# Half-size products for the first matrix product of the channel mixers' second passes

## The reference, cut to what matters

```
h   = rmsnorm(x, norm_ffn_g[layer]) * (1.0 + sc2) + sh2
hid = jnp.square(jax.nn.relu(jnp.einsum('bsd,df->bsf', h, w_ff1[layer])))   # 1024 -> 4096
x   = x + g2 * jnp.einsum('bsf,fd->bsd', hid, w_ff2[layer])                 # 4096 -> 1024
...
m = jnp.einsum('bd,de->be', jax.nn.silu(c), w) + b     # modulation: sh, sc, g for both halves of a layer
```

## Time and profile before

| | us |
|---|---|
| three timed runs | 2747.79, 2771.42, 2804.4 |
| median | 2771.42 |
| the profiled execution's own time | 2761.02 |
| its span on the slowest core (core 2) | 2759.5 |
| spans of all cores | 2687.8 to 2759.5 |
| PE / DVE / ACT / POOL busy | 2679.8 / 1831.6 / 1351.7 / 865.0 |

### The profile page before, as it was taken

One profiled execution on the slowest core, in us unless ns is written; L12 is line 12 of the kernel. 1 busy time (PEld: TensorE's weight loads), 2 busy tenths in 40 slices (PEclk: granted clock), 3 DMA queues, 4 the chain that ended last, 5 costly groups with the idle time before them and its releaser, 6 DMA issues.

```text
span 2759.5 us, 49737 instructions; the slowest of 8 cores (2687.8 to 2759.5 us)
## 1 busy us (share of the span) xinstructions
PE 2679.8 (97%) x16860; PEld 1576.9 (57%) x16860; DVE 1831.6 (66%) x3259; ACT 1351.7 (49%) x2155; POOL 865.0 (31%) x956
## 2 busy tenths in 40 slices
PE   3999999999999999999999999998999999999998
PEld 1444444445656766676675444444766666676675
DVE  3577776777656667777767666676656666666766
ACT  4787777783445443223225655544445443334323
POOL 4455555442424421000002443413423430112111
PEclk9899999999999999999999988898999999999999
DMA  9743444447453359757536556554254347222321
GB/s 191 152 124 104 108 107 108 108 108 153 105 153 96 93 154 184 173 128 173 124 95 158 153 148 171 139 135 125 77 140 136 93 139 167 83 87 77 131 84 62
DMA packets 126410, 348.12 MB, mean 126 GB/s; under 512 B 13904, under 2 KB 16464, under 8 KB 115280
## 3 DMA queue, kind: packets, MB, share of 16 engines
q1 hardware_dynamic: 107008, 266.29, 31.1%
q0 software_dynamic: 19152, 78.65, 17.6%
HBM read 301.90 MB, written 117.44 MB: 152 GB/s over the span
## 4 chain that ended last, share of the span: by engine, by line
PE 91%; DMA 3%; DVE 2%; issue 2%; ACT 1%; POOL 1%; DVEq 0%; SPq 0%; ACTq 0%; POOLq 0%
PE ps L743 47%; PE ps L1171 28%; PE ps L1011 4%; PE ps L1394 4%; PE ps L1340 4%; PE ps L984 2%; DMA sb_arena<-w_in 1%; DMA xs<-sb_arena 1%; DMA sb_arena<-xs 1%; POOL sb_arena L1387 1%; PE ps L888 0%; PE ps L1377 0%; ACT L412 0%; DVE sb_arena L1364 0%; PE ps L694 0%
## 5 line engine op out<-in xcount | busy, mean ns | idle before, releaser
L743 PE MATMUL ps<-sb_arena 128*128 128x512 bf16 x6144 | 1425.3, 390 | 5.1 <-DMA sb_arena<-w_in 5.1
L743 PEld LDWEIGHTS ps<-sb_arena 128*128 128x128 bf16 x6144 | 608.5, 100 | 733.5 <-issue 179.4
L1171 PE MATMUL ps<-sb_arena 128*128 128x256 bf16 x7168 | 804.6, 274 | 6.5 <-DVE sb_arena L1139 6.5
L1171 PEld LDWEIGHTS ps<-sb_arena 128*128 128x128 bf16 x7168 | 704.7, 98 | 108.9 <-issue 8.8
L692 POOL TENSOR_TENSOR sb_arena<-sb_arena 128x512 f32<-128x512 f32 (+1 forms) x259 | 359.9, 1390 | 968.7 <-ACT sb_arena L689 942.5
L1183 DVE SCALAR_TENSOR_TENSOR sb_arena<-ps,sb_arena 128x256 f32<-128x256 f32 x1280 | 526.7, 477 | 193.2 <-PE ps L1171 188.7
L1133 ACT ACTIVATE sb_arena<-ps 128x512 f32<-128x512 f32 x512 | 304.0, 595 | 681.0 <-PE ps L743 626.3
L1139 DVE TENSOR_TENSOR sb_arena<-sb_arena 128x512 bf16<-128x512 f32 x288 | 225.6, 783 | 336.2 <-ACT sb_arena L1133 335.8
L1152 DVE TENSOR_TENSOR sb_arena<-sb_arena 128x1024 bf16<-128x1024 bf16 x320 | 258.3, 843 | 47.5 <-ACT sb_arena L1136 39.2
L689 ACT ACTIVATE sb_arena<-sb_arena 128x512 f32<-128x512 f32 x273 | 168.0, 622 | 58.6 <-POOL sb_arena L692 32.3
L412 ACT ACT_TABLE_LOAD x124 | 159.1, 1283 | 46.0 <-PE ps L743 33.8
(11 more groups left out here) (129 smaller groups left out, 1906.1 us busy)
## 6 DMA issues: line engine op xcount, KB each, us to landing
xs<-sb_arena SPq DMA_DIRECT2D x320, 256.0 KB, 4.7
sb_arena<-xs SPq DMA_DIRECT2D x160, 512.0 KB, 6.0
sb_arena<-w_ff POOLq DMA_DIRECT2D x32, 1024.0 KB, 12.1
sb_arena<-ada_w POOLq DMA_DIRECT2D x72, 256.0 KB, 5.6
sb_arena<-x SPq DMA_DIRECT2D x64, 256.0 KB, 3.9
hs<-sb_arena SPq DMA_DIRECT2D x16, 1024.0 KB, 12.3
sb_arena<-hs SPq DMA_DIRECT2D x16, 1024.0 KB, 8.8
sb_arena<-xs SPq DMA_DIRECT2D x64, 256.0 KB, 4.1
```

The lines of the kernel that those rows point to most:

```text
L743: parts = [(lambda e, kc=kc: e.matmul(bk(B), w[:, kc, col0:col0 + 128], hT[:, kc, :], start=kc == 0, stop=kc == 7), [wb, hb[kc]], c_mm(512 ...
L1171: parts.append((lambda e, m=m, fc=fc, h=h, r=r: e.matmul(bk(Bm)[:, h * H:(h + 1) * H], w[:, fc, m * 128:(m + 1) * 128], r, start=h == 0 an ...
```

## The change

In the second pass of each layer (p = 1) the first product is made by seven half-size products as well. The K of 1024, the 2048 hidden channels and the 512 positions are each halved. `first_sums` makes the sums of the weight quarters once a pass, 10 instructions of 128x2048 elements, four of them on GpSimd. `prepare` adds 5 sums of h for each tile, in place or into a buffer `Th`. `ff1_halves` replaces `ff1`: for each of 8 pairs of output blocks a bank "grows" through three visits, with reads between them, and what has to be shared between banks is gathered in a small buffer `part`. h now lives in one buffer for all tiles, instead of two in turn.

The second pass's `ff2` is rewritten in the same per-bank form: products 2 and 5 into two halves of a bank (ScalarE copies one, VectorE adds the other), product 1 shared, then 4 with 3 and 7 with 6 onto the same bank. It has the same 224 matmuls; 24 adds into x and 8 helper adds replace the 40 adds. The first pass keeps both of its functions (the old `ff2` is called `ff2_plain`).

Around it: slots are dealt out anew, so the quarters of w_ff2 for a second pass go to slots that the pass before uses to its end, and all w_in loads of `phase_m1` come at the end of the second pass. One of the five sums of w_ff2 for a second pass moves to GpSimd. 32 of the 48 modulation vectors are made in layer 0's first pass (7 a tile), 16 in its second (4 a tile). `finish` takes channels in another order and stores some parts on ScalarE's queue. `TP` becomes 52.5 for the first and 49.0 for the second pass.

```diff
-        TP = 52.5
+        TP = (52.5, 49.0)
 
         FFS = {(0, 0): ((5, 4, 3, 6), (1, 2, 0, 9), (10, 11, 7)),
-               (0, 1): ((12, 13, 14, 15), (5, 4, 3, 6), (1, 2, 0)),
-               (1, 0): ((0, 1, 2, 4), (5, 6, 7, 9), (10, 11, 12)),
-               (1, 1): ((13, 14, 15, 3), (0, 1, 2, 4), (5, 6, 7))}
+               (0, 1): ((12, 13, 14, 15), (10, 11, 7, 9), (1, 2, 0), (5, 4, 3), 6),
+               (1, 0): ((0, 1, 2, 7), (9, 6, 12, 13), (14, 15, 10)),
+               (1, 1): ((3, 4, 5, 11), (14, 15, 10, 13), (9, 6, 12), (0, 1, 2), 7)}
+        FUSED = (0, 3)
+        FADD = 4
+        POOLED1 = ((7, 0), (6, 0), (7, 1), (6, 1))
+        POOLED2 = (7,)
...
+            return out
+
+        def first_sums(l, w1, key):
+
+            homes = FFS[l, 1][3]
+            out = {}
+            for i, home in zip((2, 5, 1), homes):
+                lo = slot_lo[home]
+                v = view(lo, [128, 2, 4, 512], BF16)
+                out[i] = [(v[:, g], G.buf("f%d_%d_%d" % (i, l, g), lo + 4096 * g, lo + 4096 * g + 4096))
+                          for g in range(2)]
+            q = {}
+            for g in range(2):
+                for name, i, h in (("11", g, 0), ("12", g, 1), ("21", 2 + g, 0), ("22", 2 + g, 1)):
+                    q[name, g] = (w1[i][0][:, 4 * h:4 * h + 4, :], w1[i][1][h])
+            for g in range(2):
+                for n, (i, x, y, op) in enumerate(((2, "21", "22", ALU.add), (5, "11", "12", ALU.add),
+                                                   (1, "11", "22", ALU.add), (7, "12", "22", ALU.subtract),
+                                                   (6, "21", "11", ALU.subtract))):
+                    d = out[i][g] if i in (2, 5, 1) else q[x, g]
+                    eng = "pool" if (i, g) in POOLED1 else "dve"
+                    G.add(eng, lambda e, d=d, x=q[x, g], y=q[y, g], op=op: e.tensor_tensor(
+                        out=d[0], in0=x[0], in1=y[0], op=op),
+                          [q[x, g][1], q[y, g][1]], [d[1]], key + 12.0 * g + 0.1 * n, 1.25 if eng == "dve" else 4.7)
+            out[7], out[6] = ([q[k, g] for g in range(2)] for k in ("12", "21"))
+            out[3], out[4] = ([q[k, g] for g in range(2)] for k in ("11", "22"))
             return out
...
+                    Th = o["Th"]
+                    for n, (dst, x, y, op) in enumerate(((Th[1], (0, 0), (1, 1), ALU.add), (Th[6], (0, 0), (0, 1), ALU.add),
+                                                         (Th[7], (1, 0), (1, 1), ALU.add),
+                                                         (None, (0, 1), (1, 1), ALU.subtract),
+                                                         (None, (1, 0), (0, 0), ALU.subtract))):
+                        xa, xbufs = hq(ti, *x)
+                        ya, ybufs = hq(ti, *y)
+                        da, dbufs = (dst[0], [dst[1]]) if dst else (xa, xbufs)
+                        dve(lambda e, xa=xa, ya=ya, da=da, op=op: e.tensor_tensor(out=da, in0=xa, in1=ya, op=op),
+                            xbufs + ybufs, dbufs, key + 30 + 0.1 * n, 0.6)
                     load(ti, key + 15, (2, 3, 0, 1), after)
...
+            def ff1_halves(ti, b):
+                flat = hid.rearrange("p a c t -> p (a c) t")
+                Th, F = o["Th"], w1
+                grow, mid, grow_ops = [None] * 8, [None] * 4, [[], [], [], []]
+
+                def product(B, col, i, m, start=False):
+                    w, wb = F[i][m // 4]
+                    parts = []
+                    if i not in Th:
+                        kh, nh = {2: (0, 0), 5: (1, 1), 3: (0, 1), 4: (1, 0)}[i]
+                        r, rb = hq(ti, kh, nh)
+                    else:
+                        r, rb = Th[i][0], [Th[i][1]] * 4
+                    for kc in range(4):
+                        parts.append((lambda e, kc=kc, r=r, w=w: e.matmul(
+                            bk(B)[:, col:col + H], w[:, kc, (m % 4) * 128:(m % 4) * 128 + 128], r[:, kc, :],
+                            start=start and kc == 0, stop=kc == 3, skip_group_check=True), [wb, rb[kc]], c_mm(H)))
+                    return parts
+
+                def part(m):
+                    v, pb = o["part"][(m // 2) % 3]
+                    return v[:, m % 2, :], pb[m % 2]
+
+                def first(m, k):
+                    B = grow[m] = bank("ff")
+                    op = pe(product(B, 0, 2, m, True) + product(B, H, 5, m), [B], k, barrier[-4:])
+                    grow_ops[m // 2].append(op)
+                    t, tb = part(m)
+                    act(lambda e: e.activation(out=t, in_=bk(B)[:, 0:H], func=AF.Copy), [B], [tb], k - 20, c_act(H, True))
+                    dve(lambda e: e.tensor_tensor(out=t, in0=bk(B)[:, H:TT], in1=t, op=ALU.add), [B, tb], [tb], k - 20,
+                        0.34)
+                    return op
...
+                def second(m, k):
+                    B, q = grow[m], m % 2
+                    pe(product(B, 0, 4, m) + product(B, H, 3, m), [B], k)
+                    act(lambda e: e.activation(out=rt[:, q, :], in_=bk(B), func=AF.Relu), [B], rtb[2 * q:2 * q + 2],
+                        k - 20, c_act(TT, True))
+                    square(rt[:, q, :], rtb[2 * q:2 * q + 2], m + 8, 8, k)
+
+                def shared(i, k):
+                    B = mid[i] = bank("ff")
+                    pe(product(B, 0, 1, 2 * i, True) + product(B, H, 1, 2 * i + 1), [B], k, grow_ops[i])
+                    for h in range(2):
+                        t, tb = part(2 * i + h)
+                        dve(lambda e, h=h, t=t: e.tensor_tensor(out=t, in0=bk(B)[:, h * H:(h + 1) * H], in1=t,
+                                                                op=ALU.subtract), [B, tb], [tb], k - 20, 0.34)
+
+                def third(m, k):
+                    B = grow[m]
+                    pe(product(B, 0, 7, m) + product(B, H, 6, m), [B], k)
+                    t, tb = part(m)
+                    z, zb = o["z"][0][:, m % 2, :], o["z"][1][m % 2]
+                    zz = z.rearrange("p (a b) -> p a b", b=H)
+                    dve(lambda e: e.tensor_tensor(out=zz, in0=bk(B).rearrange("p (a b) -> p a b", b=H),
+                                                  in1=t.unsqueeze(1).to_broadcast([128, 2, H]), op=ALU.add),
+                        [B, tb], [zb], k - 20, 0.62)
+                    if m in FUSED:
+                        dve(lambda e: e.scalar_tensor_tensor(out=flat[:, m:m + 25:24, :], in0=zz, scalar=0.0, in1=zz,
+                                                             op0=ALU.max, op1=ALU.mult), [zb],
+                            [hidb[m], hidb[m + 24]], k - 4, 0.75)
+                        return
+                    act(lambda e: e.activation(out=z, in_=z, func=AF.Relu), [zb], [zb], k - 4, c_act(TT))
+                    square(z, [zb], m, 24, k - 4)
+
+                def both(f, i, k):
+                    return [f(2 * i + h, k + 0.87 * h) for h in range(2)][0]
+
+                begun[ti] = both(first, 0, b)
+                for i in range(4):
+                    k = b + 1.73 + 6.05 * i
+                    both(second, i, k)
+                    shared(i, k + 1.73)
+                    if i < 3:
+                        both(first, i + 1, k + 2.6)
+                    both(third, i, k + 4.33)
+                    if i % 2:
+                        hidden_sums(i // 2, k + 4.33)
...
+                def first(m, k):
+                    B = grow[m] = bank("f2")
+                    two, five = product(B, 0, 2, m, True), product(B, H, 5, m)
+                    pe(two[:6] + five[:6], [B], k)
+                    pe(two[6:] + five[6:], [B], k + 5.2)
+                    act(lambda e: e.activation(out=part(m), in_=bk(B)[:, 0:H], func=AF.Copy), [B], [rtb[m]], k,
+                        c_act(H, True))
+                    dve(lambda e: e.tensor_tensor(out=part(m), in0=bk(B)[:, H:TT], in1=part(m), op=ALU.add),
+                        [B, rtb[m]], [rtb[m]], k - 6, 0.34)
...
+                def shared_product(q, k):
+                    B = bank("f2")
+                    barrier.append(pe(product(B, 0, 1, 2 * q, True) + product(B, H, 1, 2 * q + 1), [B], k))
+                    for h in range(2):
+                        m = 2 * q + h
+                        dve(lambda e, m=m, h=h: e.tensor_tensor(out=part(m), in0=bk(B)[:, h * H:(h + 1) * H],
+                                                                in1=part(m), op=ALU.subtract), [B, rtb[m]], [rtb[m]],
+                            k - 6, 0.34)
+                        for nh in range(2):
+                            add(rtb[m], lambda m=m: part(m), m + 4 * nh, nh, k + FADD)
+
+                def side(m, nh):
+                    return lambda: bk(grow[m])[:, nh * H:(nh + 1) * H]
+
+                def stage(m, kinds, k):
+                    B = grow[m]
+                    parts = []
+                    for i in kinds:
+                        parts += product(B, H if i in (3, 6) else 0, i, m)
```

(44 more changed lines are left out.)

196 lines of the change are left out of this document (121 added, 75 removed).

## The result

| | before | after |
|---|---|---|
| median, us | 2763.32 | 2809.27 |
| ratio after / before | | 1.0203 (95% interval 1.0153 to 1.0252) |
| the profiled execution's own time | 2761.02 | 2803.2 |

On another chip the same pair gave 1.0269 (1.0249 to 1.0289), 74 us above 2704. The forecast was 2724 (2680 to 2785); its sum of parts was −47 us, the profiled executions differ by +42. In the profiled execution of the kernel before one die was disturbed (2743.4 us at a granted clock of 0.967, against 2692.1 us at 0.990 on the other), and its core 2 lies on that die, so the +42 makes the loss look smaller than it is.

The account below looks back on a forecast made before the run. TensorE's own matmul stream, busy 97% of the span, was taken as the bound. Terms −50.9 + 3 + 4 − 3 = −47 us took the profiled 2761.0 to 2714; with the median 10.4 us above, 2724 us, range 2680 to 2785.

Parts of the forecast that it names:

- Modulation: Layer 0's first pass: 32 sums and their loads move in, 8.5 us of VectorE a tile; 0, bound +3 us.
- w_in of the spatial mixer: End of layer 0's second pass: four loads moved there arrive by the mixer's start or a few us after; 0, bound +8.
- Hidden by GpSimd being idle: Second pass's start: four weight sums on GpSimd, about 5.0 us each, 20 us in all, cost TensorE no wait.
- The first product: Second passes: 224 matmuls of 256 replace 128 of 512, saving 3.18 us a tile; −50.9 us over 16 tiles.
- Seams in a tile: Second-pass tiles: waits between visits to growing banks, 0.2 us a tile (bounds 0 to 4); +3 us for 16.
- the burst rival: Second visit of each pair: TensorE waits for VectorE's bursts, 2829 by the median; chance 0.08 for slower by over 2%.
- Quarters of w_ff2: Second pass's start: loads into slots freed late make the second product wait 0 to 6 us once or twice; +4 us.
- The end: After the last product: eight of 16 scalings (3.2 us) leave if half the positions are ready earlier; −3 us, bounds −5 and 0.
- The clock, a rival at 0.05: Second passes: with busier VectorE and ScalarE the granted clock falls to 0.91, +64 us, no gain, 2784; chance 0.05.
- The second sign: Second-pass stages: the prediction is wrong if TensorE's busy share there falls below 98%.

Follow-up runs that it names:

- before_mod: Kernel before with only the modulation's move: 32 of 48 vectors made in layer 0's first pass, 7 a tile; ratio 1.0182 to the kernel before.
- calm_mix: Changed kernel, constants early, weight sums on VectorE, 28 modulation vectors at first-pass mid-tile, 20 in second pass, w_ff1 loads moved off the turn; 0.9948 of before.
- mod_calm: Changed kernel with first-pass modulation loads issued behind the 13th of 16 first-product groups, sums some 20 us later, 8 places instead of 4; 1.0192 of the kernel before.
- sums_dve: Changed kernel with all sums of weights on VectorE, none on GpSimd; ratio 1.0197 to the kernel before.

## Why the prediction was wrong, step by step

- **The failed step is "Modulation: 32 of 48 sums of 1.22 move into layer 0's first pass with their loads in GpSimd's queue ... no wait there now: 0, bound +3".** It was +49 us (before_mod). I counted VectorE's 8.5 us a tile and named the queue, but priced no transfer: not what else is in flight when seven loads start. "No wait there now" was nearly true and no cover: ScalarE waited 3.8 us for x in 300 us, but one load of weights already lay on each turn, with stores landing in 9.6 us. With the modulation's loads on top the stores took 13.7, the next x came late, and ScalarE's norm, VectorE's squares and TensorE stood behind it. None of the rivals had this mechanism; the slower one named VectorE's bursts in the second pass.
- "w_in of the spatial mixer: 0, bound +8": w_in was fine (TensorE waited 6.1 us for it in the whole span on core 2, and 5.1 in the kernel before), but the small constants beside it were moved as well, and I gave them no price. They cost 14 to 19 us of tile time. A moved step has to be counted with every DMA in it, and here it was not.
- "Hidden by GpSimd being idle": wrong. Its weight sums were late and slowed VectorE: 7 us at each second pass's start, 14 in all. A row for it was there: 0.97 instead of 0.69 beside a busy GpSimd. The price of one, 5.0 us, was about right (4.7 and 6.0 in the mean); that TensorE need not wait for them was not.
- The first product, −50.9: right in the stream (109 ns), and not all of it on the path. A middle tile became 49.5 us in layer 1, that is 2.8 less, of the 3.18 − 0.2 forecast. The start of layer 1's second pass gives back 8 us; that VectorE is full there is my reading, and I had priced those sums at nothing. Layer 1 kept 14 of 25 us, layer 0 none of them before the loads were moved (calm_mix). Why layer 0's last tile and the mixer behind it are longer stays open.
- Seams in a tile, +3: L1224 waited 6.9 us in the whole span. Right in kind, half the size. VectorE was less busy than the sum had it: 119.22 of 148.40 us in three middle tiles of layer 1, 80% and not 87%, and the burst rival did not come in the middle of a pass.
- Quarters of w_ff2, +4: the wait that names their sums is 1.4 us on core 2 and 3.3 on core 1; what more of the start is theirs cannot be told from VectorE's crowd. Open.
- The end, −3: from the last second-product matmul to the end 14.6 us (the prediction has 14.9) became 12.9, so −1.7.
- The clock, a rival at 0.05: half true, but as a result, not a cause. Core 1, windows of 4 us around one wait of 4.7 us in the first pass:

```profile
784.00:788.00 4.00, 4.00 (x20) 1.82 (x19) 3.62 (x4) 3.39 (x7) 3.71 (x3) 1.00 0.01 2
788.00:792.00 4.00, 1.21 (x10) 0.69 (x7) 3.92 (x5) 2.22 (x5) 3.71 (x3) 0.95 0.00 0
792.00:796.00 4.00, 2.07 (x10) 1.46 (x11) 4.00 (x6) 0.17 (x1) 2.77 (x2) 0.50 0.02 4
796.00:800.00 4.00, 4.00 (x28) 3.09 (x26) 3.34 (x8) 0.00 (x0) 0.00 (x0) 0.69 0.00 0
800.00:804.00 4.00, 4.00 (x38) 3.48 (x37) 3.92 (x11) 1.32 (x2) 1.38 (x2) 1.00 0.00 0
```

TensorE stands still at 789 to 794 us, comes back at a granted 0.50, the lower level of 1.2 GHz, and is at 2.4 GHz again by 800. So this wait is paid twice, once as a wait and once in slow matmuls behind it; the 45 us estimated in the section on the result are the same thing over a whole core. In mod_calm, between 740 and 900 us, where TensorE has no wait, the granted clock is 1.00.

The prediction said that it was wrong if a tile took over 50 us in the chain (it took 49.5) or the stages' busy share fell below 98%: 404.08 of 420 is 96%, 407.10 is 97%. The second sign was the true one, though not of the stream itself, which was busy for 99 to 100% in the middle of both second passes.

## What to carry to other kernels

A load that moves is not only an entry in a queue: write down which transfers are in flight when it starts, and who waits for *them*. In this tiled pass, whose buffers go round, the turn of the tile (store, then load into the same home, then the first reads) could bear one more load and not several, and the middle of the tile was free. And a saving on the bounding engine was only worth its steady part: the start of a pass, which gathers new helper work on another engine, handed microseconds back, and waits cost again in the clock. Look, too, at what else an experiment moves: the places that mod_calm added held up the weights' loads, and that was part of its effect.

## What the runs showed of the hardware, unexpected

- How long a 256 KB store of x took to land hung on what was issued with it, not on the mean traffic: between 740 and 900 us, at 133 GB/s after and 136 in mod_calm, the median was 13.7 us with four to seven 256 KB loads and a 1 MB load around a turn, 9.6 with the 1 MB load alone (kernel before, 124 GB/s), and 4.9 with neither.
- After a wait of 4.7 us the granted clock was 0.50 for the next matmuls and back at 1.00 within about 6 us.
- GpSimd's 128x2048 bf16 sums took 4.7 and 6.0 us in the mean by line. Beside them VectorE's mean was 1.86 instead of 1.22 us, with half of them still at 1.22 or less and the longest at 5.08; with all sums on VectorE (sums_dve) none of that line's twenty took over 1.23.
